# First norm's factors multiplied in as a row, first slab in three pieces; branches merged ahead of splits; another order in the last attention

## The chip, the cores and the metric

The kernel runs on one core of one Trainium2 chip. The metric is the device time of one execution in microseconds. Three executions of the kernel before gave a median of 1022.47 us (1021.98 to 1023.92).

## What is computed

Three transformer layers act one after another on x of 256 tokens by 1024 columns. All arithmetic is float32.

```python
# layer 1: attention with a forgetting bias and a gated short convolution, side by side
h = rmsnorm(x, norm_mix_pre)                     # x * rsqrt(mean(x*x) + 1e-6) * g
q, k, v, f, g_b, g_c, hc, gate_conv, gate_attn = split(h @ w_in)
ya = g_b * causal_conv(g_c * hc);  yb = forgetting_attention(q, k, v, f)
merged = sigmoid(gate_conv) * (ya @ w_branch[0]) + sigmoid(gate_attn) * (yb @ w_branch[1])
x = x + rmsnorm(merged @ w_out, norm_mix_post)
x = x + rmsnorm(swiglu(rmsnorm(x, norm_ffn_pre)), norm_ffn_post)
# layers 2 and 3: scale and shift of every norm from c ("modulation"),
# attention with a bias by distance (layer 2: 8 heads of 128, called moba;
# layer 3: differential, called diff: a = softmax(s0) - lam * softmax(s1), o = a @ v,
#   o = rmsnorm(o) per head, then o @ w_o), and a swiglu after each
```

## The kernel before

**Arithmetic.** TensorE (PE) multiplies float32 as three products of rounded parts: a weight w is held as `high` (rounded) and `low` = w - high, an activation as `_hi` and `_lo`, and high*hi, low*hi and high*lo are summed. So each block of weights passes ScalarE (ACT), which rounds it (`act_round`, L490), and then VectorE (DVE), which subtracts (`dve_rest`, L496), before PE may read it.

**The slabs.** All weights stream in slabs of 128 x 2048 floats (1 MB), numbered in the order of `MAIN`: 159 of them, loaded by SyncE (SP) into eight buffers; a buffer is loaded again once PE has done with the slab in it. Between them come 48 slabs `ada` of the modulation, which DVE alone sums. ACT and DVE take the slabs in order: `act_next(name, index, ahead)` and `dve_next(...)` split all slabs up to the one that PE now works on plus `ahead` (3 by default, `FAR` = 5), and then do what stands in their list for the attention. Every engine works through one list written out by hand (functions `tensor`, `scalar`, `vector`, `gpsimd`, `sync`), strictly in its order, and waits on semaphores; the names given to `.up(...)` and `wait_ge` pair up.

**Kinds of product.** `pe_still` holds weights still and gives transposed results (two or four column blocks, a PSUM bank for two). `pe_moving` holds the activations still and gives rows of tokens: for each token tile t (two of 128), slab i and column half c, four k steps of three matmuls of 512 columns. `between` names work put after a block (t, i, c). `pe_wide` does an output projection of four slabs so, in the order 0, 2, 1, 3, and puts the transposes of the next norm's first tile (`pe_turn(stage, 0)`, L311) before its last block.

**A norm between stages** (`act_post_norm`, `dve_post_norm`): squares on ACT (L343), the product with the gain on DVE (L404), the power -1/2 on GpSimd (POOL, L355), the new x (L419), again squares and a power, the scaled x (L360), eight transposes on PE (L311), the factors and the shift on ACT (L323, L325), the split into h_hi and h_lo on DVE (L337, L339). Then the next matmuls start. This is done for tile 0 and then for tile 1.

**The start.** ACT's DMA queue loads the identity, then the right halves of both tiles of x, then small columns; SP's loads the left halves, then slab 0 in two pieces, constants and the next slabs. PE passes the time with 14 and later 10 matmuls on zeros (`keep_busy`, L1078). The first norm multiplies its factors in on ACT, as a column per block, after the transposes.

**The branches.** ACT and DVE split as far as `AHEAD + n * (half + 1)` before they merge half `half` of branch n; DVE waits for the whole slab of a branch, multiplies with the gate (L1455), adds (L1460), ACT rounds (L1272), DVE subtracts (L1463), for each of four pairs g of blocks.

**The last attention.** For head h: scores on PE (L814), bias and maximum on DVE (`dve_score_head`, L831, L840), exponentials on ACT (L848), the weights on DVE (`dve_weigh`, L855 to L871), their transposes on PE (L880), a copy on ACT (L888). Two heads at a time (`apply_pairs`, L1019 to L1021) are multiplied with the values, copied by DVE (L1036), squared in four pieces on ACT (L1029), joined (L1039), raised to a power (POOL), scaled (L1047), transposed (`turn_pairs`, L1055), and split (L894, L902). DVE's list holds copy, wait and join of a pair directly behind one another.

**The feed-forward part.** In the last group g = 10 ACT and DVE first split up to `FAR` and then do the hidden product (L745, L726, L749).

## Time and profile before

| what | value |
|---|---|
| median of three executions | 1022.47 us |
| profiled execution | 1022.51 us |
| its span, first to last instruction | 1021.0 us |
| PE busy | 995.3 us |
| DVE busy | 688.0 us |
| ACT busy | 491.4 us |

The profiled execution takes 1.5 us more than its span, for what lies before the first and after the last instruction. Where PE is busy throughout, time can only come from fewer or faster matmuls; the 25.7 us in which it is idle lie in a few stretches between stages.

### The profile page before, as it was taken

How to read it: one execution, taken by the hardware profiler on the slowest of the kernel's cores; microseconds unless marked ns; L12 is line 12 of the kernel's file. 1: busy time of each engine (PE TensorE's matmuls, PEld its weight loads, DVE VectorE, ACT ScalarE, POOL GpSimd, SP SyncE). 2: the span in 40 equal slices, each digit the busy share in tenths (PEclk: the TensorE clock that was granted, in tenths of full speed). 3: DMA queues.
4: the chain of work that ended last, by engine and by line, in shares of the span. 5: the costliest groups of instructions: out<-in, count | busy, mean ns of one | idle time of the engine just before them, and what ended most of it. 6: DMA issues, size and time to landing. Idle time of an engine off the chain costs nothing.

```text
span 1021.0 us, 16052 instructions
## 1 busy us (share of the span) xinstructions
PE 995.3 (97%) x6874; PEld 914.1 (90%) x6874; DVE 688.0 (67%) x986; ACT 491.4 (48%) x688; POOL 33.3 (3%) x51
## 2 busy tenths in 40 slices
PE   7999999899999999999999999999999899999997
PEld 6988899789898998899889999997997689999996
DVE  5766756769757768887778768667676766545443
ACT  5644544454334345555564334455667664434341
POOL 3000000010000000100000000001000010000000
PEclk9999999999999999999999999999999999999999
DMA  9663367556897775786467778875643257555511
GB/s 366 262 229 101 126 251 280 206 188 246 314 259 289 296 278 193 265 313 247 166 248 266 300 280 308 312 293 179 214 137 125 83 130 262 171 201 171 201 42 41
DMA packets 33303, 225.65 MB, mean 221 GB/s; under 512 B 3997, under 2 KB 4277, under 8 KB 6864
## 3 DMA queue, kind: packets, MB, share of 16 engines
q1 hardware_dynamic: 31104, 219.00, 59.8%
q0 software_dynamic: 1552, 4.88, 1.4%
q8 instruction: 54, 0.88, 0.3%
q10 hardware_dynamic: 576, 0.74, 0.2%
q14 instruction: 17, 0.14, 0.0%
HBM read 223.54 MB, written 1.08 MB: 220 GB/s over the span
## 4 chain that ended last, share of the span: by engine, by line
PE 88%; DVE 6%; ACT 3%; issue 1%; DMA 1%; POOL 0%; ACTq 0%; DVEq 0%
PE psum L569 18%; PE psum L571 18%; PE psum L570 18%; PE psum L595 8%; PE psum L596 8%; PE psum L597 8%; DVE low L496 2%; PE psum L814 2%; ACT high L490 1%; PE psum L659 1%; PE psum L660 1%; PE psum L661 1%; PE psum L311 1%; PE psum L880 1%; DMA x_res<-in_x 1%
## 5 line engine op out<-in xcount | busy, mean ns | idle before, releaser
L496 DVE TENSOR_TENSOR low<-raw,high 128x2048 fp32r<-128x2048 f32 (+1 forms) x160 | 362.3, 2276 | 162.7 <-ACT high L490 162.1
L569 PE MATMUL psum<-h_hi,high 128*128 128x256 f32 x1504 | 428.6, 285 | 0.0
L571 PE MATMUL psum<-h_hi,low 128*128 128x256 f32 x1504 | 425.5, 283 | 0.0
L570 PE MATMUL psum<-h_lo,high 128*128 128x256 f32 x1504 | 425.5, 283 | 0.0
L490 ACT ACTIVATE high<-raw 128x2048 fp32r<-128x2048 f32 (+1 forms) x160 | 301.0, 1899 | 53.1 <-DMA raw<-in_gate_up 27.9
L569 PEld LDWEIGHTS psum<-h_hi,high 128*128 128x128 f32 x1504 | 288.4, 192 | 5.2 <-issue 2.3
L570 PEld LDWEIGHTS psum<-h_lo,high 128*128 128x128 f32 x1504 | 288.5, 192 | 1.1
L571 PEld LDWEIGHTS psum<-h_hi,low 128*128 128x128 f32 x1504 | 288.5, 192 | 0.0
L595 PE MATMUL psum<-high,y_hi 128*128 128x512 f32 x328 | 129.1, 394 | 2.9 <-DVE y_lo L902 1.7
L596 PE MATMUL psum<-low,y_hi 128*128 128x512 f32 x328 | 128.0, 390 | 0.0
L597 PE MATMUL psum<-high,y_lo 128*128 128x512 f32 x328 | 127.7, 389 | 0.0
L505 DVE CUSTOM_DVE_ANT_0 raw<-raw,c_row 128x1024 f32<-128x1024 f32 x96 | 113.5, 1220 | 2.7 <-DMA raw<-in_ada 2.7
L719 ACT ACTIVATE work_v<-psum 128x512 f32<-128x512 f32 x30 | 17.9, 597 | 126.5 <-PE psum L571 126.5
L726 ACT ACTIVATE y_hi<-work_v 128x512 fp32r<-128x512 f32 x30 | 19.0, 632 | 122.2 <-DVE work_v L745 122.2
L595 PEld LDWEIGHTS psum<-high,y_hi 128*128 128x128 f32 x328 | 61.7, 188 | 15.7 <-issue 2.0
L597 PEld LDWEIGHTS psum<-high,y_lo 128*128 128x128 f32 x328 | 61.6, 188 | 13.1
L596 PEld LDWEIGHTS psum<-low,y_hi 128*128 128x128 f32 x328 | 61.7, 188 | 11.5
L595 PE MATMUL psum<-high,h_hi 128*128 128x512 f32 x112 | 45.4, 405 | 4.3 <-DVE h_lo L1463 3.3
L596 PE MATMUL psum<-low,h_hi 128*128 128x512 f32 x112 | 43.7, 390 | 0.0
L597 PE MATMUL psum<-high,h_lo 128*128 128x512 f32 x112 | 43.7, 390 | 0.0
L355 POOL TENSOR_TENSOR stat<-stat,minus_half 128x1 f32<-128x1 f32 x24 | 13.4, 560 | 801.5 <-DVE stat L349 801.5
L745 DVE TENSOR_TENSOR work_v<-psum,work_v 128x512 f32<-128x512 f32 x30 | 20.7, 691 | 25.1 <-PE psum L571 25.1
(173 smaller groups left out, 904.7 us busy)
## 6 DMA issues: line engine op xcount, KB each, us to landing
raw<-in_gate_up SPq DMA_DIRECT2D x66, 1024.0 KB, 5.1
raw<-in_ada SPq DMA_DIRECT2D x48, 1024.0 KB, 6.4
raw<-in_down SPq DMA_DIRECT2D x33, 1024.0 KB, 5.3
raw<-in_mix SPq DMA_DIRECT2D x14, 1024.0 KB, 5.1
raw<-in_moba_qk SPq DMA_DIRECT2D x8, 1024.0 KB, 7.2
raw<-in_diff_qk SPq DMA_DIRECT2D x8, 1024.0 KB, 6.2
raw<-in_qk SPq DMA_DIRECT2D x4, 1024.0 KB, 14.7
raw<-in_branch SPq DMA_DIRECT2D x4, 1024.0 KB, 6.1
```

The costliest lines, as they stand in the source:

```text
L490: nc.scalar.activation(high[n % N_HI][:, s], raw[i % N_RAW][:, s], ACT.Copy).then_inc(*rounded.up(n if key is None else key))
L496: nc.vector.tensor_tensor(low[i % N_RAW][:, s], raw[i % N_RAW][:, s], high[n % N_HI][:, s].bitcast(F32), ALU.subtract).then_inc(*rest.up(key))
L505: last = nc.vector.tensor_tensor_reduce(out=w, in0=w, in1=c_row[:, :], scale=1.0, scalar=0.0, op0=ALU.mult, op1=ALU.add, accum_out=mod_raw ...
L569: nc.tensor.matmul(to, a, hi(k), start=first, stop=False)
L570: nc.tensor.matmul(to, a, lo(k), start=False, stop=False)
L571: m = nc.tensor.matmul(to, r, hi(k), start=False, stop=last and j > j0)
L595: nc.tensor.matmul(psum[b][:, :], hi(k0 + k, t), vh, start=first, stop=False)
L596: nc.tensor.matmul(psum[b][:, :], hi(k0 + k, t), vl, start=False, stop=False)
L597: m = nc.tensor.matmul(psum[b][:, :], lo(k0 + k, t), vh, start=False, stop=last)
L726: nc.scalar.activation(y_hi[:, 2 * (g % 4):2 * (g % 4) + 2, :], ffn_tmp(g)[:, 1], ACT.Copy).then_inc(*hi_made.up(("hidden", f, g)))
L745: nc.vector.tensor_tensor(ffn_tmp(g)[:, 1], pair(bank_of[*up, 0]), ffn_tmp(g)[:, 0], ALU.mult).then_inc(*produced.up(("hidden", f, g)))
L814: m = nc.tensor.matmul(o[:, w], q[:, tile_of(t)], k[:, 0:(t + 1) * P], start=True, stop=more is None)
```

## The change

The start: x's right half leads ACT's queue, slab 0 comes in three pieces over both queues, the constants go behind slab 2; the factors of the first norm are loaded as one row by GpSimd, spread over the partitions by two matmuls with a row of ones, and multiplied in by DVE with the scale; ACT then rounds and DVE subtracts directly from the transposed block in PSUM.

```diff
+        FIRST = [(0, 2), (2, 4), (4, 8)]
+        def act_first(t, a, b):
+            yield from act.wait_ge(turned, ("in", t, a))
+            nc.scalar.activation(h_hi[:, a:b, tile_of(t)], first_of(t, a, b), ACT.Copy)...
+        def dve_first(t, a, b):
+            yield from dve.wait_ge(hi_made, ("in", t, a))
+            nc.vector.tensor_tensor(h_lo[...], first_of(t, a, b), h_hi[...].bitcast(F32), ALU.subtract)...
+        def dve_scale_first(t):
+            yield from dve.wait_ge(powed, ("x", "in", t))
+            for c in range(2):
+                yield from dve.wait_ge(small_pe, ("row", c))
+                nc.vector.scalar_tensor_tensor(
+                    out=work_a[:, half_of(t, c)], in0=x_res[:, t, c * 512:(c + 1) * 512], scalar=stat[:, 2 * t:2 * t + 1],
+                    in1=psum[5 + 2 * c][:, :], op0=ALU.mult, op1=ALU.mult)...
+        FIRST_PIECES = [slice(0, 512), slice(512, 1024), slice(1024, SLAB)]
 tensor:
-            keep_busy(14)
-            yield from pe_turn("in", 0)
-            keep_busy(10)
+            keep_busy(5)
+            ... # wait for the row; for c in 0, 1: matmul(psum[5 + 2 * c], ones, row half c)
+            keep_busy(2)
+            yield from pe_first(0)
+            keep_busy(5)
 scalar:
+            nc.scalar.dma_start(x_res[:, 0, 512:], ...); ident; raw[0][:, second]; x_res[:, 1, 512:]; wf_raw; cols
             act_square(x_res[:, 0, 0:512], ("x", "in", 0, 0), 0, 0, 0)
+            ... # round pieces 0 and 1
             yield from act.wait_ge(x_in[1], "left", "right")
+            for c in range(2):
+                act_square(x_res[:, 1, c * 512:(c + 1) * 512], ("x", "in", 1, c), 1, c, 0)
+            for a, b in FIRST[:2]:
+                yield from act_first(0, a, b)
+            yield from act_round(0, 0, FIRST_PIECES[2], (0, 2))
+            yield from act_first(0, *FIRST[2])
 vector:
+            yield from dve_scale_first(0)
+            ... # rest piece 0, first (0, 2), join 1, rest piece 1, first (2, 4), rest piece 2, scale 1, first (4, 8), then tile 1
```

The branches, the output projections and the feed-forward part:

```diff
 pe_still:
-            m.then_inc(*slab.up(n, (name, index), *alias))
+                done = j0 + 2 == n_chunks
+                m.then_inc(*slab.up((name, index, b), *((n, (name, index), *alias) if done else ())))
 scalar and vector:
-                    yield from dve_next("branch", 2 * n + half, AHEAD + n * (half + 1))
+                    yield from dve_next("branch", 2 * n + half, AHEAD + (half if n == 0 else 0))
-                        yield from dve.wait_ge(slab, ("branch", 2 * n + half))
+                        yield from dve.wait_ge(slab, ("branch", 2 * n + half, b))
 pe_wide:
-            turn = {(1, 0, 1): lambda: pe_turn(stage, 0)}
+            turn = {(1, 2, 1, 1): lambda: pe_turn(stage, 0)}    # inside the last block, after its second k step
 act_ffn and dve_ffn:
-                yield from dve_next(*up, AHEAD if g < FG - 1 else FAR)
+                yield from dve_next(*up)
                 ... # the hidden product
-                if g < FG - 2:
-                    yield from dve_next(down, base * FG + g - 1)
+                yield from dve_next(*((down, base * FG + g - 1) if g < FG - 2 else (*up, AHEAD if g < FG - 1 else FAR)))
```

The last attention (slabs 122 to 125 are those of the output projection):

```diff
 scalar, from head 4 on:
-                            yield from act_apply_pairs((0, 4))
+                            yield from act_exp(*act_behind.pop(0))
+                            yield from act_split(NUM[tag + "_qk", 7] + AHEAD + 1)      # to slab 123
 ...
+                    act_apply_pairs(0); act_exp 5; act_turn_probs 4; act_exp 6, 7; act_turn_probs 5
+                    act_apply_pairs(2); act_turn_probs 6; act_values(v, 1); act_turn_probs 7; act_turn_pairs(0, 2)
+                    yield from act_apply_pairs(4, 6)
+                    yield from act_next(v, 3)                                          # slab 124
+                    yield from act_turn_pairs(4)
+                    yield from act_next("diff_o", WIDE[0])                             # slab 125
+                    yield from act_turn_pairs(6)
 vector:
+                    dve_join_pair(0); weigh 5; dve_score_head 6, 7; weigh 6; dve_copy_pair(2); weigh 7
+                    dve_scale_pairs(0); dve_join_pair(2); dve_scale_pairs(2); dve_turn_pairs(0, 2)
+                    yield from dve_copy_pair(4)
+                    yield from dve_copy_pair(6)
+                    yield from dve_next(v, 3)                                          # slab 124
+                    yield from dve_join_pair(4)
+                    yield from dve_join_pair(6)
+                    yield from dve_scale_pairs(4, 6)
+                    yield from dve_turn_pairs(4)
+                    yield from dve_next("diff_o", WIDE[0])                             # slab 125
+                    yield from dve_turn_pairs(6)
 tensor:
+                    turn_probs 4; values(2) with score_head 6 inside; score_head 7; apply_pairs 2; turn_probs 5
+                    values(3) with turn_probs 6 inside; turn_probs 7; turn_pairs(0, 2)
-                    yield from pe_apply_pairs((4, None), (6, None))
-                    yield from pe_wide("diff_o", y_tok, rows, behind, {}, {(0, 0, 1): lambda: pe_turn_pairs(4, 6)})
+                    yield from pe_wide("diff_o", y_tok, rows, behind,
+                                       {(0, 0, 0): late_values, (1, 0, 0): lambda: pe_turn_pairs(4)}, {(0, 0, 1): lambda: pe_turn_pairs(6)})
```

`late_values` is `pe_apply_pairs((4, None), (6, None))`.

## Rows read from the trace of the kernel before

**Rows 1.** Windows view: engine busy time (instructions), granted clock, DMA share, GB/s.

```profile
0.00:20.00 20.00, 14.26 (x79) 13.20 (x80) 9.06 (x24) 8.71 (x23) 8.31 (x13) 0.91 0.90 352
180.00:212.00 32.00, 27.83 (x145) 22.86 (x144) 24.66 (x31) 14.77 (x26) 1.12 (x2) 1.00 0.52 187
...
765.00:813.00 48.00, 42.03 (x250) 34.71 (x250) 33.47 (x106) 32.18 (x89) 4.06 (x4) 0.96 0.33 110
sum 1021.00, PE 995.33 PEld 914.14 DVE 687.96 ACT 491.45 POOL 33.30; mean PE 66.36 PEld 60.94 DVE 45.86 ACT 32.76 POOL 2.22
```

**Rows 2.** Waits of PE: for whom, us in total, times, longest.

```profile
PE psum L311 <- DVE work L360: 6.1, 3, 4.3
PE psum L880 <- DVE prob L871: 4.3, 3, 2.5
PE psum L595 <- DVE h_lo L1463: 3.3, 3, 1.3
PE psum L595 <- DVE y_lo L902: 1.7, 1, 1.7
PE psum L595 <- DVE y_lo L749: 1.2, 1, 1.2
```

**Rows 3.** Timeline of the start: start, us, instruction, [idle before, releaser].

```profile
6.05 0.69 DVE L1344 CUSTOM_DVE_ANT_0 work_v<-x_res 128x512 f32<-128x512 f32 x1 [5.06 <-DMA x_res<-in_x]
8.75 0.63 ACT L343 ACTIVATE work_v<-x_res 128x512 f32<-128x512 f32 x1 [1.98 <-DMA x_res<-in_x]
...
11.22 3.98 PE L1078 MATMUL psum<-prob_t 128*128 128x128 f32 x20
...
19.24 0.50 PE L595 MATMUL psum<-high,h_hi 128*128 128x512 f32 x1 [0.39 <-DVE h_lo L339]
```

**Rows 4.** Windows view of three stretches with and without PE work.

```profile
4.30:6.00 1.70, 1.67 (x15) 1.48 (x14) 0.00 (x0) 0.00 (x0) 0.00 (x0) 1.00 0.98 319
...
11.20:14.50 3.30, 3.30 (x18) 3.30 (x17) 2.83 (x6) 3.01 (x10) 3.30 (x2) 0.50 1.00 422
...
796.20:799.60 3.40, 3.40 (x16) 3.21 (x17) 1.63 (x5) 1.01 (x3) 0.00 (x0) 0.50 0.04 14
```

**Rows 5.** Timeline of ACT and DVE around the branches.

```profile
173.37 1.92 ACT L490 ACTIVATE high<-raw 128x2048 fp32r<-128x2048 f32 x1 [6.05 <-DMA raw<-in_out]
182.24 0.68 DVE L1455 TENSOR_TENSOR bias<-psum,bias 128x512 f32<-128x512 f32 x1
204.32 0.69 DVE L404 TENSOR_TENSOR work<-psum,gain 128x512 f32<-128x512 f32 x1
```

**Rows 6.** Timeline of DVE at the second feed-forward part's end.

```profile
685.82 6.70 DVE L496 TENSOR_TENSOR low<-raw,high 128x2048 fp32r<-128x2048 f32 x3 [2.63 <-ACT high L490]
692.43 0.68 DVE L745 TENSOR_TENSOR work_v<-psum,work_v 128x512 f32<-128x512 f32 x1
...
697.83 0.69 DVE L404 TENSOR_TENSOR work<-psum,gain 128x512 f32<-128x512 f32 x1
```

**Rows 7.** Timeline of the last attention's end, all engines.

```profile
799.57 0.69 DVE L1036 COPY work<-psum 128x512 f32<-128x512 f32 x1 [1.73 <-PE psum L1021]
802.03 0.17 DVE L1039 TENSOR_SCALAR diff_stat<-diff_stat 128x4 f32<-128x4 f32 x1 [1.77 <-ACT lam_pr L1029]
804.44 3.71 ACT L490 ACTIVATE high<-raw 128x2048 fp32r<-128x2048 f32 x2
805.86 0.88 DVE L1047 TENSOR_SCALAR work<-work,diff_stat 128x128 f32<-128x128 f32 x4 [0.35 <-POOL diff_stat L355]
817.22 0.68 DVE L404 TENSOR_TENSOR work<-psum,gain 128x512 f32<-128x512 f32 x1
822.20 0.39 PE L596 MATMUL psum<-low,y_hi 128*128 128x512 f32 x1
822.43 0.39 PE L597 MATMUL psum<-high,y_lo 128*128 128x512 f32 x1
822.74 1.06 PE L311 MATMUL psum<-const,work 128*128 128x128 f32 x8
```

More of the change, by code:

```diff
@@ L308, in pe_turn @@
                     yield from pe.wait_ge(ident_in, "ident")
-                    yield from pe.wait_ge(*((scaled_pool, k // 4) if stage == "in" and t else (scaled, (stage, t, k // 4))))
+                    yield from pe.wait_ge(scaled, (stage, t, k // 4))
                     at = t * D + k * P
@@ L334, in dve_split_h @@
             yield from dve.wait_ge(affined, (stage, t, b - 1))
-            if stage != "in":
-                yield from dve.wait_ge(slab, H_USED[stage][t])
+            yield from dve.wait_ge(slab, H_USED[stage][t])
             nc.vector.tensor_copy(h_hi[:, s, w], work_b[:, s, w]).then_inc(*h_hi_made.up((stage, t, a)))
@@ L486, in act_round @@
         def act_round(i, n, s=slice(0, SLAB), key=None):
-            yield from act.wait_ge(*((raw_first, "a") if key == (0, "a") else (raw_in[i % N_RAW], i)))
+            yield from act.wait_ge(*((raw_in[i % N_RAW], i) if key in (None, (0, 2)) else (raw_first[key[1]], key)))
             if n >= N_HI:
@@ L581, in pe_moving @@
                     seen.add(i)
-                    yield from pe.wait_ge(rest, (0, "a") if n == 0 else n)
+                    yield from pe.wait_ge(rest, (0, 0) if n == 0 else n)
                 wh = high[n % N_HI][:, :].rearrange("p (k n) -> p k n", k=kcs)
@@ L588, in pe_moving @@
                 for k in range(kcs):
-                    if n == 0 and k == kcs // 2:
-                        yield from pe.wait_ge(rest, n)
+                    if n == 0 and k in (1, 2):
+                        yield from pe.wait_ge(rest, (0, k))
                     for signal, key in ready(k0 + k, t):
@@ L597, in pe_moving @@
                     m = nc.tensor.matmul(psum[b][:, :], lo(k0 + k, t), vh, start=False, stop=last)
+                    if (t, i, c, k) in between:
+                        yield from between[t, i, c, k]()
                 done = t == NT - 1 and c == blocks[-1]
@@ L721, in act_ffn @@
                     yield from act_turn_rows(f)
-                yield from act_next(*up, AHEAD if g < FG - 1 else FAR)
+                yield from act_next(*up)
                 yield from act.wait_ge(produced, ("hidden", f, g))
@@ L727, in act_ffn @@
                     *hi_made.up(("hidden", f, g)))
-                if g < FG - 2:
-                    yield from act_next(down, base * FG + g - 1)
+                yield from act_next(*((down, base * FG + g - 1) if g < FG - 2 else (*up, AHEAD if g < FG - 1 else FAR)))
             yield from act_next(down, base * FG + FG - 1)
@@ L1024, in act_apply_pairs @@
         def act_apply_pairs(*pairs):
-            for h, _ in pairs:
+            for h in pairs:
                 yield from act.wait_ge(produced, ("o", h))
@@ L1267, in scalar @@
                 for half in range(2):
-                    yield from act_next("branch", 2 * n + half, AHEAD + n * (half + 1))
+                    yield from act_next("branch", 2 * n + half, AHEAD + (half if n == 0 else 0))
                     for g in (2 * half, 2 * half + 1) if n else ():
@@ L1350, in vector @@
-            yield from dve.wait_ge(squared_dve, 0)
+            nc.vector.memset(prob_t[0][0:1, P:2 * P], 1.0).then_inc(*small_dve.up("ones"))
+            yield from dve.wait_ge(x_in[0], "left", "right")
+            x = x_res[:, 0, 512:]
+            nc.vector.tensor_tensor_reduce(
+                out=work_v[:, 0, 512:], in0=x, in1=x, scale=1.0 / D, scalar=0.0, op0=ALU.mult, op1=ALU.add,
+                accum_out=stat[:, 1:2]).then_inc(*squared_dve.up("right"))
+            yield from dve.wait_ge(squared_dve, "right")
@@ L1351, in vector @@
             yield from dve_join(("x", "in", 0), 0, 0)
-            yield from dve.wait_ge(x_in[1], "left", "right")
-            square_right(1)
-            yield from dve.wait_ge(squared_dve, 1)
+            yield from dve_scale_first(0)
+            for i, kind, m in dve.items(0):
+                yield from dve_rest(0, 0, FIRST_PIECES[0], (0, 0))
+            yield from dve_first(0, *FIRST[0])
             yield from dve_join(("x", "in", 1), 1, 0)
-            yield from dve_scale_x("in", 0)
@@ L1519, in gpsimd @@
         def gpsimd():
+            nc.gpsimd.dma_start(gain[2][0:1, :], dram["mix_pre"]).then_inc(*row_in.up("row", by=16))
             nc.gpsimd.memset(minus_half[:, :], -0.5).then_inc(*small_pool.up("halves"))
```

179 lines of the change are left out of this document (96 added, 83 removed).

## Prediction

> **What bounds the kernel now.** I read the windows view first. PE is busy 995.3 of 1021.0 us [rows 1]; nearly all of the 25.7 us of idle time lies at the start (5.7 of the first 20 us), around the branches and the first output projection (4.2 of 32 us) and in the last attention (6.0 of 48 us). Elsewhere PE works without a gap, and the change touches no matmul there. So each part is worth what it does to these holes, and to the small ones at the ends of the feed-forward parts. The waits of PE name what ends each [rows 2]: the first transposes wait 4.3 us for DVE's scaled x, two other transposes share 1.8 us, the merged h_lo costs 3.3, the weights of the last attention 4.3, its y_lo 1.7, the last hidden product of the first feed-forward part 1.2. Two stretches run at half clock, 1.2 in place of 2.4 GHz: 11.2 to 14.5 and 796.2 to 799.6 [rows 4]. PE has little slack against DVE in the norms: the transposes of the last wide norm start at 822.74, right as PE arrives (its last matmul began at 822.43) and as the scaled x is there [rows 7]. So a PE that arrives sooner gains nothing in a norm unless DVE and ACT arrive sooner too. That is my test for each part.
>
> **Part 1, the start.** Now tile 0 of x is there at 6.05 and tile 1 at 8.75; zeros at half clock (20 pieces, 3.98 us from 11.22) occupy PE until 15; tile 1's matmuls start at 19.24 [rows 3]. *x tile 0*: its right half no longer stands behind the identity, nor its left beside it: I estimate 4.7 (bounds 3.9 and 6.05). It turns out not to matter, because ACT's list puts both squares of tile 1 ahead of the first `act_first`. *x tile 1*: on ACT's queue it now has 576 KB ahead of it in place of 320, on SP's 512 in place of 256. 256 KB more at 319 GB/s [rows 4] is 0.8 us: 9.4 (bounds 7.5, if the small first pieces pay, and 10). From there: two squares 1.45, rounding 0.35, subtraction 0.4, with 0.3 of signalling: tile 0's first matmul at 11.9, without zeros in the way. The next k step needs the second piece's rest (12.5); the third waits for piece three: ACT rounds it to 12.6, DVE subtracts from 12.85 to 14.0. Behind that DVE scales tile 1 (two products with a PSUM operand, by L404's 0.69 [rows 5]), so its transposes start at 15.5, and through rounding and subtraction its matmuls start at 16.8 against 19.24. The f logits and slab 1 follow 2.6 earlier than before, and slab 1's split (ACT from 17.05, DVE to 21.2) is ready 1.1 before need. What keeps it from being more is DVE: nothing else in its list may be late. The row itself (4 KB on GpSimd's queue, two matmuls with one row of ones) lies under the wait for x and the power. With x tile 1 at 7.5 the gain would be 4.2, at 10.0 it would be 2.0. The clock is the other unknown. PE now gets 5 + 2 + 5 zero matmuls in place of 24, and the stretch before the first product has waits in it. The rows show that the clock held after 1.67 us of work in 4.30:6.00 and fell after an idle stretch that ended in transposes alone [rows 3, 4]. At half clock for 3.4 us the gain shrinks by 0.4 only (PE waits for DVE there anyway); for twice as long it shrinks to 0.6. I take -2.3, bounds -4.2 and 0.
>
> The page "TensorE: Matmul & The Clock Gate" of the Trainium skill says (Part 4: PE-mode transpose) that transposes do not count as work for the clock in the way matmuls do. Both falls here have transposes right before them, so the trace agrees. By it the new start, with few matmuls between transposes, would sit at half clock at least once, and this rule speaks for the smaller gain, -2.2 down to -0.6.
>
> **Part 2, the branches.** Now DVE subtracts two more slabs before it merges (merge at 182.24, though branch 2 is finished at 179.7), and again before the second half; PE waits 3.3 us in the middle of the projection [rows 2, 5]. In the new order slab 25 comes before the second half of branch 0 is merged: it lands at 173.37 [rows 5], so DVE is through with it at 177.5 and with that merge at 178.8 (branch 3 needs those banks at 179.7: 0.9 to spare). Then four merges at 2.7 us each (three operations of 0.69 and 0.6 for ACT between): h_lo is complete for k 0 to 3 at 184.1, before PE arrives at 185.3; slab 26 takes DVE to 187.6, and the other two merges end at 190.3 and 193.0. PE needs them at 193.5. The 3.3 us go. Next late is slab 27: rounded only after the last merge, it is ready at 196.4 and costs PE 0.3. But DVE still has slabs 27 to 30 ahead of the norm, and the norm's first product starts at 203.0 in place of 204.32 [rows 5]: DVE's list holds as much work, only its waits for ACT shrink from 6.4 to 5.1 us. So the transposes of tile 0 start at 208.2 (209.5 before), PE having waited 2.0 for them. With the turn inside the last block six matmuls stand behind it in place of twelve, so PE is through 2.6 earlier, and the first rows of the next stage wait 0.2 for h_lo. Tile 1's norm follows tile 0's: -2.1, bounds -2.7 and -1.0.
>
> The same placement of the turn in the second projection: PE waits 0.9 there now. The new place is 0.46 later than the end of that wait; the matmuls behind it are finished sooner, but h_lo of k 4 to 7 follows the transposes by 4.75 us and is then the last to come: +0.3 (bounds 0 and +0.5). In the third this chain is inside part 4.
>
> **Part 3, the feed-forward ends.** In the first one PE's wait of 1.2 [rows 2] goes, but ACT now rounds slabs 61 and 62 only after the hidden product, DVE idles 1.1 us for it, and the norm starts when it did (400.4): PE waits those 1.2 at the transposes instead. +0.1. In the second there is no wait to remove. DVE does three slabs from 685.82 to 692.5, then the product, and the norm's product starts at 697.83 [rows 6]. In the new order the hidden product is finished at 691.2; slabs 110 to 112 follow (6.7 us, the first one rounded at 692.3): 698.95. The transposes, now exactly on time at 703.04, come 1.1 later. +1.1 (bounds 0 and 1.3). The third has no slabs behind it.
>
> **Part 4, the last attention.** The new order hides the weights well: turns of head 4 at once, 0.6 for head 6, about 1.0 at the rows, in place of 4.3 [rows 2]; and the half clock of 796.2 goes with it (1.7 us [rows 4]). The product of pair 6 ends 2.8 us sooner, at 798.2. But then PE's list has only twelve moving matmuls (0.23 apart [rows 7], 2.7 us) before `turn_pairs(4)`, where it had thirty-six. And pair 4's rows are scaled late: copy of pair 6 0.7, four squares 1.77 [rows 7], then slab 124, which stands between on both lists: ACT 1.86 (half of 3.71), DVE 2.25; two joins 0.25, the power 1.1 (804.57 + 0.17 to 805.86), the scale 0.4, signals 0.5: 8.8 us. PE waits 6.0. That pair 4's own squares are finished 1.8 us sooner does not help, since slab 124 waits for pair 6's. Afterwards DVE has the same four slabs and four y_lo left before the norm as before (10.6 us), 1.2 of it waiting for ACT, whose rounding of 125 and 126 stands behind y_hi of pairs 4 and 6. The norm starts at 819.9 against 817.22 [rows 7]: +2.7. A hole of 6 us brings the half clock, as 2.5 us of idling before transposes did now: the matmuls of slab 123's tile 0, and so rows 6 and 7 and all of ACT's and DVE's list behind, come another 1.1 to 2.6 later. I take +1.7. Sum +4.4. Below it is bounded by +2.5 (no half clock), above by +5.4. The old waits of 4.3 and 1.7 are in this: what was five small holes is one large one.
>
> **The sum.** Against the profiled execution's 1022.51 (span 1021.0 and 1.5 around it; the median of three is 1022.47, so nothing to correct): -2.3 - 2.1 + 0.3 + 0.1 + 1.1 + 4.4 = +1.5. 1024.0 us.
>
> **Rivals.** *The attention pays* (0.19): if ACT and DVE are so far ahead that slab 124 does not hold up the pair, the hole is 2 us and the norm starts with PE's arrival; part 4 is then about -2, the total 1022.5 - 2.3 - 2.1 + 0.3 + 0.1 + 1.1 - 2 = 1017.6. For it speaks that DVE idles some 3 us before pair 4's product; against it that both lists put slab 124 behind the pair. *The clock takes it all* (0.19), on the slower side: half clock over two stretches of 3.4 us at the start and again over 5 us after the hole: -0.6 - 2.1 + 1.5 + 5.4 = +4.2, 1026.7. It decides from the point where the stretch after 11.1 or after the hole stays at 0.5 beyond 3.4 us. *The branch gain is swallowed* (0.12): if slab 25 or the banks of branch 3 are late, DVE's norm starts at 204.3 as now; part 2 is 0 to -0.6, the total 1026.
>
> **Chances.** My forecast's own case has 0.50 and spans 1021.5 to 1026. What a measurement here can tell from no change is 0.2%, 2.0 us: 1020.4 to 1024.5. Of the forecast 0.36 is within, 0.12 slower, 0.02 faster; the first rival gives 0.19 faster, the clock 0.19 slower, the swallowed branch half to each of within and slower. Faster 0.21, same 0.42, slower 0.37. The range, 1018.5 to 1027, leaves out a tenth on each side.
>
> **What would show it.** Right: tile 1's first v1 matmul near 16.8; no wait of PE on L1463's successor and a wait of 2 us at the first projection's transposes; the hidden wait of the first feed-forward part gone and its transposes no earlier; one idle stretch of some 6 us on PE ahead of the rows of head 4, ended by DVE's scale, with slab 124's round and rest in front of it, and a granted clock of 0.5 behind. Wrong: that hole under 3 us, or the last norm's product earlier than 817.22 less what was gained before it; the second norm's product (203.0) not moved; x tile 1 landing before 8 us.

## The result, and the profile of the changed kernel

The changed kernel takes 1026.69 us (median of 7 runs, 1025.87 to 1027.68); the kernel before took 1023.92 in the 7 runs beside it (1021.98 to 1025.66). The ratio is 1.0031, 95% interval 1.002 to 1.0042: slower by 0.3%. I had forecast 1024.0, with no measurable change as the likeliest outcome (0.42). The time lies inside the range and at the figure of the rival "the clock takes it all" (1026.7), but not for that rival's reason.

The profiled execution has a span of 1025.3 us against 1021.0. Between the two profiled executions the change is 4.2 us, between the medians 2.8: the profiled execution of the kernel before (1022.51), on which I had built the forecast, is 1.4 us under its median. The table below explains the 4.2. The windows that answer to [rows 1] (columns as there):

```profile
0.00:20.00 20.00, 15.63 (x60) 11.91 (x61) 9.01 (x19) 8.54 (x18) 4.67 (x12) 1.00 0.93 343
180.00:212.00 32.00, 29.87 (x160) 25.11 (x159) 24.52 (x30) 17.41 (x29) 1.11 (x2) 1.00 0.64 233
765.00:813.00 48.00, 40.47 (x242) 33.42 (x241) 30.66 (x104) 28.08 (x85) 4.03 (x4) 0.93 0.31 109
```

And PE's waits over the whole span, which answer to [rows 2]:

```profile
PE psum L308 <- DVE work L389: 6.9, 4, 2.0
PE psum L1089 <- DVE work L1081: 6.8, 2, 6.2
PE psum L1120 <- DMA gain<-in_mix_pre: 3.0, 1, 3.0
PE psum L913 <- DVE prob L904: 0.8, 1, 0.8
```

The waits for merged h_lo (3.3) and for the hidden product (1.2) are gone, those for the last attention's weights fell from 4.3 to 0.8. In their place stand one wait of 6.2 at the last attention's transposes (the hole), one of 3.0 for the new row, and four at the norms' transposes.

To find where the time went I compare the two timelines at the first matmul of each stage. These rows of PE are of the changed kernel: slab 1 of the first projection, then the first matmul behind the first projection and its norm, behind the first feed forward, behind the second projection, behind the second feed forward, and in the last feed forward.

```profile
24.73 0.40 PE L628 MATMUL psum<-high,h_hi 128*128 128x512 f32 x1
...
218.17 0.36 PE L694 MATMUL psum<-high,h_hi 128*128 128x256 f32 x1 [0.48 <-DVE h_lo L368]
...
414.14 0.50 PE L628 MATMUL psum<-high,h_hi 128*128 128x512 f32 x1 [0.28 <-DVE h_lo L368]
...
521.26 0.35 PE L694 MATMUL psum<-high,h_hi 128*128 128x256 f32 x1 [0.57 <-ACT work L322]
...
712.97 0.50 PE L628 MATMUL psum<-high,h_hi 128*128 128x512 f32 x1 [0.28 <-DVE h_lo L368]
...
837.68 0.35 PE L694 MATMUL psum<-high,h_hi 128*128 128x256 f32 x1 [0.57 <-ACT work L322]
```

And the same of the kernel before:

```profile
24.87 0.40 PE L595 MATMUL psum<-high,h_hi 128*128 128x512 f32 x1
...
220.48 0.35 PE L659 MATMUL psum<-high,h_hi 128*128 128x256 f32 x1 [0.48 <-DVE h_lo L339]
...
416.40 0.50 PE L595 MATMUL psum<-high,h_hi 128*128 128x512 f32 x1 [0.28 <-DVE h_lo L339]
...
523.34 0.36 PE L659 MATMUL psum<-high,h_hi 128*128 128x256 f32 x1 [0.57 <-ACT work L325]
...
713.86 0.50 PE L595 MATMUL psum<-high,h_hi 128*128 128x512 f32 x1 [0.28 <-DVE h_lo L339]
...
833.76 0.36 PE L659 MATMUL psum<-high,h_hi 128*128 128x256 f32 x1 [0.47 <-ACT work L325]
```

The change of each stretch is the difference of two neighbouring differences. "Turn" is the early transposing of the next norm's first tile inside an output projection (`pe_turn(stage, 0)`), which the change puts later:

| stretch | forecast | measured | from |
|---|---|---|---|
| start, to slab 1 | -2.3 | -0.14 | 24.73 - 24.87 |
| branches and first projection | -2.1 | -2.17 | 193.44 - 195.61 |
| first feed forward | +0.1 | +0.05 | 195.97 - 195.92 |
| second projection (turn) | +0.3 | +0.18 | 107.12 - 106.94 |
| second feed forward | +1.1 | +1.19 | 191.71 - 190.52 |
| last attention and projection | +4.4 | +4.81 | 124.71 - 119.90 |
| behind PE's last matmul | 0 | +0.4 | 5.5 - 5.1 |
| sum | +1.5 | +4.3 | |

Four terms came within 0.12 us, the last attention within 0.41. The start gave nothing of its 2.3 us. Its timeline, PE first and then ACT and DVE:

```profile
6.59 3.75 PE L1120 MATMUL psum<-gain,prob_t 1*128 1x512 f32 x4 [3.03 <-DMA gain<-in_mix_pre]
11.28 1.91 PE L335 MATMUL psum<-const,work 128*128 128x128 f32 x8
12.99 2.17 PE L1112 MATMUL psum<-prob_t 128*128 128x128 f32 x10
14.92 0.48 PE L628 MATMUL psum<-high,h_hi 128*128 128x512 f32 x1
19.07 0.50 PE L628 MATMUL psum<-high,h_hi 128*128 128x512 f32 x1 [0.28 <-DVE h_lo L347]
```

```profile
10.92 0.63 ACT L372 ACTIVATE work_v<-x_res 128x512 f32<-128x512 f32 x1 [1.56 <-DMA x_res<-in_x]
12.16 0.63 ACT L343 ACTIVATE h_hi<-psum 128x256 fp32r<-128x256 f32 x2
```

```profile
8.76 0.75 DVE L354 SCALAR_TENSOR_TENSOR work<-x_res,stat,psum 128x512 f32<-128x512 f32 x1 [2.66 <-PE psum L1120]
12.55 0.42 DVE L347 TENSOR_TENSOR h_lo<-psum,h_hi 128x256 fp32r<-128x256 f32 x1 [0.83 <-ACT h_hi L343]
```

The row arrives at 6.45, and its four matmuls take 3.75 us, so DVE's scale stands 2.66 us behind them: it did not "lie under the wait for x and the power". x tile 1 lands at 10.9, not 9.4, and ACT's first rounding follows its squares at 12.16. Then five zero matmuls (ten pieces, 2.17 us) delay the first product to 14.92, and twelve products later tile 1 starts at 19.07, where it did before (19.24 [rows 3]).

One reading needs care. The windows view gives a granted clock of 1.00 for all of this start:

```profile
6.50:10.30 3.80, 3.71 (x5) 1.19 (x5) 0.75 (x1) 0.88 (x2) 0.26 (x1) 1.00 1.02 387
```

Yet the same four row matmuls take 3.75 us here and 1.98 in e4 below, the same eight transposes 1.91 and 1.07. Where I speak of the half rate at the start, it is read from such durations and not from the clock column; no run shows why the two differ.

The last attention went as described. ACT, DVE, POOL and PE around the hole, in order of time:

```profile
800.73 1.89 ACT L519 ACTIVATE high<-raw 128x2048 fp32r<-128x2048 f32 x1
802.65 2.29 DVE L528 TENSOR_TENSOR low<-raw,high 128x2048 fp32r<-128x2048 f32 x1 [4.03 <-ACT high L519]
805.10 1.98 POOL L384 TENSOR_TENSOR diff_stat<-diff_stat,minus_half 128x4 f32<-128x4 f32 x2 [14.30 <-DVE diff_stat L1073]
806.15 1.85 DVE L1081 TENSOR_SCALAR work<-work,diff_stat 128x128 f32<-128x128 f32 x8 [1.05 <-POOL diff_stat L384]
806.78 1.09 PE L1089 MATMUL psum<-const,work 128*128 128x128 f32 x4 [6.15 <-DVE work L1081]
```

Slab 124's round and rest (800.73 to 804.9) stand between the squares and the join. Windows behind the hole, and behind the 2.0 us wait at the last norm's transposes, show the half clock:

```profile
806.80:810.10 3.30, 3.30 (x10) 2.71 (x11) 1.99 (x8) 2.63 (x3) 0.29 (x1) 0.50 0.00 0
827.30:830.60 3.30, 3.30 (x12) 2.72 (x11) 1.91 (x7) 3.04 (x9) 0.00 (x0) 0.50 0.77 323
```

### The profile page after: what moved, and what is told of

It reads as the page before. It is cut to its first block, busy times and chain, and to the rows that moved or that the text cites. A ratio compares the mean times of both kernels' runs of the same rounds, so it can differ in the third digit from the quotient of the medians.

```text
span 1025.3 us, 15998 instructions
## 1 busy us (share of the span) xinstructions
PE 997.3 (97%) x6854; PEld 913.9 (89%) x6854; DVE 686.6 (67%) x978; ACT 489.3 (48%) x681; POOL 29.6 (3%) x50
## 4 chain that ended last, share of the span: by engine, by line
PE 87%; DVE 6%; ACT 3%; issue 2%; DMA 1%; POOL 0%; DVEq 0%; ACTq 0%; POOLq 0%
PE psum L601 18%; PE psum L603 18%; PE psum L602 18%; PE psum L628 8%; PE psum L629 8%; PE psum L630 8%; DVE low L528 3%; PE psum L847 2%; ACT high L519 1%; PE psum L694 1%; PE psum L695 1%; PE psum L696 1%; PE psum L913 1%; ACT work L322 1%; PE psum L308 1%
## 5 line engine op out<-in xcount | busy, mean ns | idle before, releaser
L629 PEld LDWEIGHTS psum<-low,y_hi 128*128 128x128 f32 x328 | 62.3, 190 | 11.6
## 6 DMA issues: line engine op xcount, KB each, us to landing
raw<-in_gate_up SPq DMA_DIRECT2D x66, 1024.0 KB, 5.0
raw<-in_ada SPq DMA_DIRECT2D x48, 1024.0 KB, 5.2
raw<-in_down SPq DMA_DIRECT2D x33, 1024.0 KB, 5.1
raw<-in_mix SPq DMA_DIRECT2D x14, 1024.0 KB, 5.0
raw<-in_moba_qk SPq DMA_DIRECT2D x8, 1024.0 KB, 7.3
raw<-in_diff_qk SPq DMA_DIRECT2D x8, 1024.0 KB, 6.0
raw<-in_qk SPq DMA_DIRECT2D x4, 1024.0 KB, 16.8
raw<-in_branch SPq DMA_DIRECT2D x4, 1024.0 KB, 5.9
```

Source lines behind the costliest of these rows:

```text
L629: nc.tensor.matmul(psum[b][:, :], hi(k0 + k, t), vl, start=False, stop=False)
```

## The experiments

Twelve kernels. e1, e2, e11 and e12 were timed in five rounds; each of the others stands on one profiled execution, which I read stretch by stretch. "Slab 1" is the first matmul of slab 1 (24.87 before, 24.73 changed).

**e1: the last attention as before.** `act_apply_pairs`, `dve_apply_pairs` and the three lists of the last attention are put back.

```diff
-                    yield from pe_turn_probs(tag, 4)
-                    yield from values(2, {(0, 0, 1): lambda: pe_score_head(tag, 6)})
...
+                    yield from pe_attend(tag, 6)
+                    yield from values(2, {(0, 0, 1): lambda: pe_attend(tag, 7)})
```

> The changed kernel with the last attention's order put back as in the kernel before (heads' weights, norms, turns, one split behind each); start, branches and feed forwards stay changed. Theory (the last attention cost 4.8 us, 1.7 of them by the low clock behind the 6.15 us hole): about 4.8 us under the changed kernel, so 1021.9, ratio to the kernel before 0.998 to 0.999; no hole over 3 us in the last attention. Rival (the loss is spread, the late shift would appear in the tail anyway, for instance as later post norm): no more than 2.5 us under the changed kernel.

1023.2 us, 0.999 of before (0.9979 to 1.0001), span 1021.8, 3.5 under the changed kernel. By stretch it is more: 713.60 to 834.15 is 120.55 against 124.71, so 4.2 us; this run's start was later (slab 1 at 25.50). The theory held, 0.6 short: the old attention with the turn's new place takes 0.65 longer than the 119.90 of the kernel before. The changed kernel without this part is no slower than the one before.

**e2: the start as before.**

```diff
-            yield from pe_first(0)
-            keep_busy(5)
+            yield from pe_turn("in", 0)
+            keep_busy(10)
```

> The changed kernel with the start put back as in the kernel before (first norm's factors by ScalarE's affine copies out of the turned tile, first slab in two halves, 14 and 10 zero products); the rest stays changed. Theory (the new start gave 0.14 us at slab 1's first product and nothing later): 1026.7 to 1026.9, the same as the changed kernel. Rival (the new start hides a loss behind slab 1, in later transfers that it moved): 0.5 us or more under the changed kernel. Rival of my forecast (the start did give 2.3 us, and something else took them): 2 us over the changed kernel, near 1029.

1027.01 us, 1.0042 (1.0028 to 1.0056), span 1025.4: the same as the changed kernel, as expected. Slab 1 is at 25.53. Over the runs with the old start it is at 24.87 and 25.53, with the new one as given at 24.73 (changed), 25.50 (e1), 25.17 (e7), 24.71 (e8), 24.72 (e10) and 24.86 (e11). The new start is worth nothing within that spread of 0.8 us.

**e3: the row on ScalarE's queue, first.**

```diff
-            nc.gpsimd.dma_start(gain[2][0:1, :], dram["mix_pre"]).then_inc(*row_in.up("row", by=16))
...
         def scalar():
+            nc.scalar.dma_start(gain[2][0:1, :], dram["mix_pre"]).then_inc(*row_in.up("row", by=16))
```

> The changed kernel with the factors' row loaded as the first transfer of ScalarE's queue instead of GpSimd's. Theory (the 3.0 us wait of the row's products is GpSimd's late transfer): the row lands before 4.5 us and its four matmuls end before 8 us instead of 10.34. Whether the first product comes earlier than 14.92 then tells two causes apart: if the turned halves alone were late, it comes at about 12.5; if ScalarE's squares of tile 1, queued ahead of its first rounding of the turned half and waiting for x tile 1 (10.9 us), hold it too, it stays at 14.5 to 15. I lean to the second, 6 to 4. Total within 1.5 us of the changed kernel.

1030.66 us, one run, span 1029.1: 2.5 us outside what I had allowed. The row's matmuls did end by 7.3 us (they began at 3.49). ACT in this kernel:

```profile
13.91 0.63 ACT L372 ACTIVATE work_v<-x_res 128x512 f32<-128x512 f32 x1 [2.54 <-DMA x_res<-in_x]
...
15.15 0.64 ACT L343 ACTIVATE h_hi<-psum 128x256 fp32r<-128x256 f32 x2
```

The transposes were finished at 10.8, yet the first rounding waited until 15.15: x tile 1, now fifth on this queue in place of fourth, landed at 13.9. So the row was not what held the first product in this kernel; ACT's own order was. Here no wait lies between the five zeros and the row's matmuls, and these still take 3.78 us, the transposes 1.94: PE works without a gap from 1.06 to 8.4 us and stays at the half rate.

**e4: fourteen zeros.** `keep_busy(5)` ahead of the row's matmuls becomes `keep_busy(14)`.

> The changed kernel with 14 zero products ahead of the row's products instead of 5. Theory (TensorE stays at the lower clock until 14.86 because it stood idle for 3 us after five zeros): the granted clock is full from about 4.3 us on, the row's four matmuls take about 1.9 us instead of 3.75 and end at 8.4 to 8.6, the eight transposes of tile 0 about 1.0 instead of 1.9 us. The first product stays at 14.5 to 15 if ScalarE's wait for x tile 1 holds it; it comes at 13 or earlier if the clock alone held it. Rival: the clock stays at half in spite of the zeros, because the wait for the row still lies behind them.

1027.95 us, span 1026.6. The row's matmuls took 1.98 us, the transposes 1.07, as the theory had it, though the row's matmuls ended at 9.3 and not at 8.6, since the zeros ran to 7.3. The first product came at 14.21, held by ACT (x tile 1 at 12.0), and ran at half clock. The windows:

```profile
6.50:9.00 2.50, 2.50 (x9) 1.27 (x7) 0.45 (x1) 0.72 (x2) 0.38 (x1) 1.00 1.00 363
9.00:11.00 2.00, 2.00 (x15) 1.78 (x15) 1.65 (x3) 0.54 (x1) 0.00 (x0) 0.91 1.06 436
...
14.20:17.60 3.40, 3.38 (x8) 2.72 (x9) 3.40 (x6) 1.26 (x3) 3.06 (x5) 0.52 1.03 424
```

The clock fell though PE was busy from 1.06 to 13.0, at 10.6, behind row matmuls and transposes. Slab 1 is at 25.54: the faster row and transposes alone gain nothing.

**e5: tile 1 of x ahead of the slab's pieces,** and **e6: the same with fourteen zeros.** In both queues x tile 1 changes places with the piece in front of it:

```diff
-            nc.scalar.dma_start(raw[0][:, second], dram["v1"][0][:, second]).then_inc(*raw_first[1].up((0, 1), by=16))
             nc.scalar.dma_start(x_res[:, 1, 512:], dram["x"][tile_of(1), 512:]).then_inc(*x_in[1].up("right", by=16))
+            nc.scalar.dma_start(raw[0][:, second], dram["v1"][0][:, second]).then_inc(*raw_first[1].up((0, 1), by=16))
```

> The changed kernel with tile 1 of x ahead of the first slab's first two pieces in the transfer queues (SP: x tile 0, x tile 1, first piece, third; ScalarE: x tile 0, identity, x tile 1, second piece); nothing else changed. Theory (two causes hold the start together: ScalarE's squares wait for x tile 1, and TensorE's row products and transposes run at the lower clock until 13.2 us): x tile 1 lands near 8.7 instead of 10.9 and the squares end before 10.5, but the transposes still end near 13, the first product stays at 14 to 15 and tile 1's first product at 18 to 19.2; no more than 1 us gained at slab 1's first matmul. Rival (the late tile alone): first product near 12.5, slab 1's first matmul 2 us earlier than 24.73.

> The same order of transfers, and 14 zero products ahead of the row's products instead of 5. Theory: with both causes gone the start gives what I forecast for it. Row's products at the full clock, ended near 8.8; transposes of tile 0 ended near 10.5; first rounding at about 10.3, first product near 11.3, tile 1's first product near 16.4 and slab 1's first matmul near 22.3 instead of 24.73. Rival (a further wait stands behind these, VectorE's rests of the first slab for instance): slab 1's first matmul at 24 or later, and one wait of 1 us or more in front of tile 1's products.

Both missed: 1029.48 and 1029.62 us, slab 1 at 27.13 and 27.16, 2.4 later than changed. In e6, ACT waits for the piece that was moved back:

```profile
7.93 0.63 ACT L519 ACTIVATE high<-raw 128x512 fp32r<-128x512 f32 x1 [2.04 <-DMA raw<-in_v]
13.04 0.63 ACT L519 ACTIVATE high<-raw 128x512 fp32r<-128x512 f32 x1 [4.48 <-DMA raw<-in_v]
...
14.80 0.63 ACT L343 ACTIVATE h_hi<-psum 128x256 fp32r<-128x256 f32 x2
```

The clock fell in e6 too, and there before the first transpose; ahead of it stand only the row's matmuls (6.46 to 8.44) and four pieces of zeros:

```profile
8.80:8.90 0.10, 0.10 (x3) 0.10 (x2) 0.10 (x1) 0.00 (x0) 0.00 (x0) 0.86 0.81 330
8.90:9.40 0.50, 0.50 (x5) 0.50 (x4) 0.50 (x2) 0.00 (x0) 0.00 (x0) 0.50 1.09 448
```

```profile
8.96 1.92 PE L335 MATMUL psum<-const,work 128*128 128x128 f32 x8
```

I had overlooked that the second piece's round stands ahead of the squares too. Whatever is fourth on ACT's queue lands at 10.9 to 13.0, and the first rounding of h stands behind it. Moving transfers only chooses which one is late; ACT's list has to change.

**e7: slab 124's split ahead of the norms.**

```diff
+                    yield from act_next(v, 3)
                     yield from act_apply_pairs(4, 6)
-                    yield from act_next(v, 3)
...
+                    yield from dve_next(v, 3)
                     yield from dve_copy_pair(4)
                     yield from dve_copy_pair(6)
-                    yield from dve_next(v, 3)
```

> The changed kernel with the second slab of the last projection's wide set (round on ScalarE, rest on VectorE) put ahead of the copies and squares of heads 4 to 7 instead of between squares and sums. Theory (the 6.15 us hole is 4.1 us of this split standing in the norms' way, and the rest their own chain): the round runs at 793 to 797 in ScalarE's gap of 4.5 us, the scales come 3.5 to 4.2 us earlier, the hole is 1.9 to 2.7 us, the clock stays full behind it, and the start of the last feed forward (837.68) comes 4.5 to 6 us earlier. Rival (the norms' own chain, or the next slabs' splits, fills the time): less than 2.5 us earlier.

1020.18 us, one run, span 1018.8, 6.5 under the changed kernel. PE's waits from 770 to 845, against 6.8 and 2.0 in the changed kernel:

```profile
PE psum L1089 <- DVE work L1081: 1.7, 2, 1.1
PE psum L308 <- DVE work L389: 1.3, 1, 1.3
```

The round now runs at 792.79, in ACT's gap. The hole is 1.12 us in place of 6.15, and every window from 796 to 840 has a granted clock of 1.00. The stretch is 118.09 against 124.71: -6.6. Of this, 5.0 lies before the transposes of pair 4, which is the hole. From them to the last norm's transposes it is 18.3 against 19.7 us, 1.35 less, with the half clock gone; from there to the last feed forward 0.3 less. The theory's mechanism held; I had put the gain at 6 at most.

**e8: the branches as before.** `AHEAD + (half if n == 0 else 0)` becomes `AHEAD + n * (half + 1)` on ACT and DVE, and the merge waits for the whole slab again.

> The changed kernel with the branches' splits and waits of the kernel before (merges wait for a whole slab, splits ahead of merges). Theory (the branches gave 2.2 us): the end of the first projection, read at the wait of its last transposes' rows (218.17 less the start's own shift), comes 2.0 to 2.4 us later; the two 1 us waits near 188 and 198 return. Rival (the earlier turn in the first projection gave part of it): 1 us or less.

1028.81 us, one run, span 1027.5. The three waits came back, 3.3 us together. But the stretch is 219.78 - 24.71 = 195.07, only 1.6 longer than changed, not 2.0 to 2.4: between theory and rival. PE has no wait at the turn here.

**e10: feed-forward ends and turn as before,** on top of e7.

```diff
-            turn = {(1, 2, 1, 1): lambda: pe_turn(stage, 0)}
+            turn = {(1, 0, 1): lambda: pe_turn(stage, 0)}
```

> The kernel with the split ahead of the norms (e7), with the feed forwards' last splits in the order of the kernel before, and the wide projections' early turn of tile 0 at its old place (ahead of the second wide slab). The two lie in different stretches. Theory for the feed forwards: the first changes by less than 0.1 us, the second comes out 1.1 to 1.2 us shorter (the wait of 1.5 us at the last attention's first transposes near 702 goes). Theory for the turn: the first projection loses up to 0.5 us (its wait of 1.86 us at the turn comes as a wait of about 1 us elsewhere), the second gains 0.2 to 0.3, the third loses nothing that I can price, within 0.5 either way. Span 1017.0 to 1018.2. Rival: the 1.2 us of the second feed forward was a wait that the late turn itself made, so neither edit alone brings it back; then undone together they still do, and the two waits near 403 go as well.

1021.85 us, span 1020.5, 2.3 over the top of what I expected. The second feed forward is 1.2 shorter (190.52 against 191.69), as said; the first is shorter by 0.65, which I had not expected (195.32 against 195.97). The turn was priced wrongly. The first projection ends 2.5 us later (220.35 - 24.72 = 195.63, against 193.15 in e7), the third stretch is 1.6 longer (119.68 against 118.09). Windows at the turn of the first and of the third projection:

```profile
204.00:207.80 3.80, 0.67 (x3) 0.20 (x2) 2.16 (x5) 1.96 (x6) 0.59 (x2) 1.00 0.54 166
207.90:211.20 3.30, 3.30 (x15) 2.76 (x16) 2.59 (x8) 2.18 (x8) 0.00 (x0) 0.68 1.00 417
820.40:823.60 3.20, 3.20 (x12) 2.91 (x13) 2.02 (x6) 2.13 (x7) 0.00 (x0) 0.52 1.02 430
```

PE waits 3.2 and 2.6 us here, and the clock falls behind both (0.68, 0.52); in e7 it waits 1.8 and 1.3, and stays at 1.00. With e8 this gives the first projection's stretch four ways:

| | old turn | new turn |
|---|---|---|
| old branches | 195.61 (before) | 195.07 (e8) |
| new branches | 195.63 (e10) | 193.44 (changed), 193.15 (e7) |

Neither half of the edit is worth more than 0.5 us alone; both together give 2.2 to 2.5. The three cases with something old stand on one execution each; the eleven profiled executions with both new lie between 193.0 and 193.4. With the new branches alone, the 3.3 us of waits at the merges are gone, but PE reaches the turn early and waits 3.2 us there in place of 0.9, and the half clock follows. The later turn gives it matmuls for part of that time.

**e9: ACT's and DVE's order at the start,** on top of e7, with 14 zeros ahead of the row's matmuls and 8 ahead of tile 1's transposes.

```diff
                 yield from act_round(0, 0, FIRST_PIECES[0], (0, 0))
                 yield from act_round(0, 0, FIRST_PIECES[1], (0, 1))
+            for a, b in FIRST:
+                yield from act_first(0, a, b)
+            yield from act_round(0, 0, FIRST_PIECES[2], (0, 2))
             yield from act.wait_ge(x_in[1], "left", "right")
```

> The kernel with the split ahead of the norms (e7), and in it the start's order changed with the changed kernel's own transfers: ScalarE rounds the turned halves of tile 0 ahead of the third piece and of tile 1's squares, VectorE's sum of tile 1's norm stands behind the first slab's rests, 14 zero products ahead of the row's and 8 ahead of tile 1's transposes. Theory (what held the first product in the changed kernel and in the three kernels with other starts is ScalarE's own queue: the first rounding of the turned half stood behind the work on the last transfer of its queue, which landed at 10.9 to 13.9): first product at 10.6 to 12, tile 1's first product near 17 (x tile 1 lands near 11 to 12, squares, power, scale and transposes behind it take 5 us), slab 1's first matmul near 22.9 instead of 24.73 to 25.2, total 1.5 to 2.5 us under e7's span of 1018.8. Rival (low clock: as in e4 it falls to half near 10.8 whatever was done before): tile 0's twelve products take 5 us instead of 2.8, tile 1's come at 18 to 19, and the gain is under 1 us.

1019.33 us, span 1018.0, 0.8 under e7; slab 1 at 24.32. The rounding came at 9.64, but the first product only at 12.67 and tile 1's at 18.69: the clock fell at 9.4 (the rival had it near 10.8), and the zeros that I had put in stood in the way.

```profile
9.64 0.81 ACT L343 ACTIVATE h_hi<-psum 128x256 fp32r<-128x256 f32 x2 [0.18 <-PE psum L335]
```

```profile
10.67 2.30 PE L1112 MATMUL psum<-prob_t 128*128 128x128 f32 x10
12.67 0.53 PE L628 MATMUL psum<-high,h_hi 128*128 128x512 f32 x1
...
15.59 1.95 PE L1112 MATMUL psum<-prob_t 128*128 128x128 f32 x16
```

**e11: e7 with the old feed-forward ends.** The order of `act_ffn` and `dve_ffn` is that of before, the turn stays new.

> The changed kernel with the split ahead of the norms (e7) and the feed forwards' last splits in the order of the kernel before; the early turn stays at its new place. Theory (e10 against e7, stretch by stretch: first feed forward 0.6 us shorter, second 1.2, and its other 4 us lost in the first and third projection belong to the turn alone): span 1017.0 against e7's 1018.8, time near 1018.4, ratio to the kernel before 0.994 to 0.996. Rival (the 0.6 us of the first feed forward came from the late start of its first projection, not from its own order): 1.2 us only, span 1017.6.

1018.02 us, ratio 0.9947 (0.9933 to 0.996), span 1016.9. First feed forward 195.40 (-0.6 against e7), second 190.51 (-1.2).

**e12: e11 with the start's order.** As e9, with one zero matmul behind tile 0's transposes and none ahead of tile 1's.

> The same, with the start's order of e9, but one zero product behind tile 0's transposes in place of five and none ahead of tile 1's transposes. Theory (in e9 the zeros stood in the way of the first product by 1.1 us, tile 1's transposes by 1.9: the scaled half of tile 1 was ready at 15.4): first product at 10.9 to 11.6, tile 1's first product at 16.5 to 17.2 instead of 18.69, slab 1's first matmul 2 us or more ahead of e9's, total 2.0 to 3.3 us under e11, near 1015.5, ratio to the kernel before 0.991 to 0.993. Rival (the half clock comes with the wait ahead of tile 1's transposes and stays): 1 us or less under e11.

1015.55 us, ratio 0.9926 (0.9913 to 0.9938), span 1014.0: 2.5 under e11 and some 11 under the changed kernel.

```profile
10.94 0.77 PE L628 MATMUL psum<-high,h_hi 128*128 128x512 f32 x1
...
15.40 1.32 PE L335 MATMUL psum<-const,work 128*128 128x128 f32 x8
16.78 0.50 PE L628 MATMUL psum<-high,h_hi 128*128 128x512 f32 x1
```

Slab 1 is at 22.42, 2.4 us earlier than in e11 (24.86), with x tile 1 landing later (12.3) than in the changed kernel. That 16.78 is the 16.8 of the forecast is luck: there tile 0's first product came at 11.9, behind tile 1's squares, and here at 10.94, ahead of them. The order and the zeros changed together. e9, with the same order and more zeros, has slab 1 at 24.32, so 1.9 us of the difference to e12 belong to twelve zero matmuls; neither the order alone nor fewer zeros alone in the changed kernel was run.

## Why the prediction was wrong, step by step

**Part 1 failed.** Of the 2.8 us by which the sum is off (+4.3 against +1.5) it accounts for 2.2. I wrote -2.3; it measured -0.14, known within the 0.8 us by which the start varies. With -2.3 the profiled execution would have come out 2.2 us lower, at 1024.5, against the forecast's 1024.0. The step that failed is the chain to tile 0's first product, which I put at 11.9 and which came at 14.92. Three of its terms were off.

- "256 KB more at 319 GB/s [rows 4] is 0.8 us: 9.4". x tile 1 landed at 10.9 in the first trace and at 11.6 to 12.3 in e4, e1, e9 and e12, outside my bounds (7.5 and 10). The 319 GB/s [rows 4] are what all queues moved together, and both ACT's and SP's queue had 256 KB more ahead of tile 1. So I should have added 512 KB, 1.6 us, and by my own rate come to 10.4. In my own chain the landing at 10.9 alone takes the gain from 2.3 to 0.8. Nor was the rate reached at first: the stretches 1.0 to 4.5 and 4.5 to 6.5 moved 187 and 227 GB/s in e4, 211 and 271 in e12.
- "without zeros in the way". h_lo was ready at 12.97 and the transposes done at 13.19, but the five zeros behind them held PE to 14.92, 1.7 us more. From there the chain is PE's own: twelve products, tile 1's transposes, 19.07. I had given the zeros no time at all, though they stand in the diff.
- "The row itself ... lies under the wait for x and the power." It landed 5.2 us after its issue, and its four matmuls with one row took 3.75 us, behind five zeros; with 14 zeros ahead they took 1.98 (e4). They ended at 10.34, when the power was long done (6.76). This held the transposes to 13.19. The page "DMA: Bandwidth & Descriptors" of the Trainium skill (Anatomy of one DMA) puts the fixed cost of a GpSimd transfer at about 2 us; this one, of 4 KB beside others, took 5.2, and the trace decides.

I did name what ties the start to x tile 1: ACT's list puts both squares of tile 1 ahead of `act_first`. I took it as harmless because I held x tile 1 to be early. e3, e5 and e6 show that ACT's list holds the first rounding at 14.8 us or later whichever transfer comes last. Its new order gave 0.85 us with the zeros left in (slab 1 at 25.17 in e7, 24.32 in e9) and 2.4 with them out (e11, e12). What either would give alone in the changed kernel stays open.

**Part 2 was right in size.** -2.17 against -2.1. The norm's first product came at 202.87 (I said 203.0), the wait at the transposes was 1.86 (I said 2.0). I had counted the later turn into this term, but had not seen that neither works without the other: e8 and e10 show that new branches alone give 0 and the new turn alone 0.5.

**The second projection and part 3** were right between the two kernels (+0.18 and +1.24 for the feed forwards, +0.3 and +1.2 forecast). The reason for the second feed forward stands: undone, it gives back 1.2 (e10, e11). For the first I had +0.1; undone it gives 0.6. The wait at the last hidden product, 1.2 us in the kernel before, is only 0.6 in e10 and 0.7 in e11, so something else in the change, which no run isolates, had already taken 0.5 of it.

**Part 4 was right in mechanism and nearly in size:** a hole of 6.15 (6.0 forecast) behind slab 124's split, with a clock of 0.50 behind it, +4.81 against +4.4. The second half-clock stretch, behind the 2.0 us wait of the last norm, I had not counted, and it cost little: from those transposes to the last feed forward it is 11.2 us in the changed kernel, and 10.9 in e4, e5 and e6, where the same wait left the clock at 1.00. e7 shows the cause of the hole directly. The rival "the attention pays" is what e7 is: had the split stood ahead of the norms, it would have been 118.09 against 119.90 before, -1.8 where I wrote -2.

**The rival "the clock takes it all"** has the right time by another road: the attention lost 4.8 and not 5.4, and the start gained 0.14 and not 0.6. The half rate was there at the start, longer than the rival had it, but it was not what decided: in e4 the row's matmuls and the transposes ran at the full rate, and slab 1 came no earlier.

**The idle time was misread.** The three stretches that I named hold 15.9 of PE's 25.7 us of idle time, not nearly all of it. 5.1 us lie behind the last matmul and 4.7 in small waits elsewhere. No term of the sum hangs on this but the one that I left out:

**The tail, +0.4, was in no term.** DVE's last product starts 0.07 us behind GpSimd's power in the kernel before and in e2, and 0.43 to 0.45 in the changed kernel and e7. But it starts 0.08 us behind in e8 too, and there the tail is as long. From PE's last matmul to the end it is 5.1 us in before and e2, 5.5 to 5.6 in every kernel with the new start. No run says why.

## What to carry to other kernels

- At a start, write down each engine's list with the landing of the transfer each item needs. An item that needs the last transfer of a queue must stand behind everything that does not; reordering the transfers under an unchanged list only changed which one was last (e3, e5, e6).
- Between two halves of a norm's chain (squares, join) put no split of a weight slab. The same split cost 5 us of hole there; 8 us earlier, where ScalarE was idle, the longest new wait of PE is 0.5 us.
- Price edits to one stretch together: removing waits paid nothing until the dependent transposes were moved back as well. And give filler matmuls a term of their own in the sum: five cost 1.7 us in the changed kernel, twelve 1.9 between e9 and e12.

## What the runs showed of the hardware that I had not expected

- The granted clock fell to 0.5 with PE busy throughout, behind 2 us of one-row matmuls: at 8.9 us in e6, 9.2 in e12, 9.4 in e9 and 10.6 in e4. The page "TensorE: Matmul & The Clock Gate" of the Trainium skill (Part 4: PE-mode transpose) says that transposes do not count as work in the way matmuls do. These falls are not shown to come from that: in e6 the clock fell before the first transpose, in e12 and e9 0.1 to 0.2 us behind it, in e4 0.9. The one-row matmuls are the likelier cause, and e3 fits, but no run replaces them with full ones.
- Waits of PE that ended in transposes were followed by the half clock at 2.5 us (the kernel before, ahead of 796.2), 2.6 and 3.2 (e10) and 6.2, and not at 1.1 to 1.9 (e7). At 2.0 us it went both ways: the same wait at the last norm's transposes was followed by 0.50 in the changed kernel, e2, e3 and e8, and by 1.00 in e4, e5 and e6. In e4:

```profile
828.80:832.10 3.30, 3.29 (x21) 2.56 (x19) 1.90 (x7) 3.30 (x10) 0.00 (x0) 1.00 1.00 365
```

- The start varies from run to run by up to 0.8 us with the same transfers in the same order (slab 1 at 24.71 to 25.50; x tile 1 landing at 10.9 to 12.3), as much as an edit there may be worth.
